# Where the moving operand of the 272-token matmuls begins within a 256-byte line

## What is computed

```python
h = concat([meta, x])                                                  # 272 tokens
h = h + 0.5 * rmsnorm(swiglu(rmsnorm(h, gn[0]), w_in[0], w_out[0]), gn[1])
h = h + rmsnorm(mlstm_mixer(rmsnorm(h, gn[2]), ...), gn[3])
h = h + 0.5 * rmsnorm(swiglu(rmsnorm(h, gn[4]), w_in[1], w_out[1]), gn[5])
return h[:, 16:]                                                       # 256 tokens
```

## Time and profile before

| what | value |
|---|---|
| median of three runs | 775.6 us (775.16 to 777.53) |
| the profiled execution's own time | 775.25 us |
| its span, first to last instruction | 773.4 us |
| TensorE busy | 765.1 us, 99% of the span |
| VectorE, ScalarE, GpSimd busy | 75%, 54%, 16% |
| mean granted TensorE clock | 0.998 of full speed |
| share of 16 DMA engines, weights' queue | 61.6% |

### The profile page before, as it was taken

One profiled execution on the slowest core, in us unless ns is written; L12 is line 12 of the kernel. 1 busy time (PEld: TensorE's weight loads), 2 busy tenths in 40 slices (PEclk: granted clock), 3 DMA queues, 4 the chain that ended last, 5 costly groups with the idle time before them and its releaser, 6 DMA issues.

```text
span 773.4 us, 14578 instructions
## 1 busy us (share of the span) xinstructions
PE 765.1 (99%) x5754; PEld 722.8 (93%) x5754; DVE 579.8 (75%) x926; ACT 417.2 (54%) x735; POOL 123.1 (16%) x140
## 2 busy tenths in 40 slices
PE   9999999999999999999999999999999999999997
PEld 9999999999999999889999998889999988999985
DVE  6877776699697887588888888677676768567663
ACT  7544444444357576495445443556655457455541
POOL 3800000032230002000000000010054411035510
PEclk9999999999999999999999999999999999999999
DMA  9867666696617564468888786735574571754541
GB/s 349 307 246 248 240 218 232 216 334 208 189 57 259 182 197 145 138 220 309 318 279 310 275 299 214 229 135 190 145 239 137 163 271 44 242 181 135 151 124 54
DMA packets 46402, 162.98 MB, mean 211 GB/s; under 512 B 5200, under 2 KB 6768, under 8 KB 46336
## 3 DMA queue, kind: packets, MB, share of 16 engines
q1 hardware_dynamic: 46336, 162.06, 61.6%
HBM read 160.96 MB, written 1.08 MB: 210 GB/s over the span
## 4 chain that ended last, share of the span: by engine, by line
PE 89%; DVE 5%; ACT 2%; issue 2%; DMA 1%; SPq 0%; POOL 0%; DVEq 0%; POOLq 0%; ACTq 0%
PE ps L374 21%; PE ps L375 20%; PE ps L376 20%; PE ps L824 5%; PE ps L826 5%; PE ps L825 5%; PE ps L766 3%; DVE w L1248 2%; PE ps L681 1%; DVE cv L1553 1%; PE ps L625 1%; PE ps L756 1%; ACT w L875 1%; PE ps L737 1%; PE ps L746 1%
## 5 line engine op out<-in xcount | busy, mean ns | idle before, releaser
L1248 DVE TENSOR_TENSOR w<-raw,w 128x1024 fp32r<-128x1024 f32 x237 | 287.9, 1222 | 124.5 <-ACT w L875 123.9
L374 PE MATMUL ps<-u,w 128*128 128x256 f32 (+1 forms) x1275 | 362.9, 285 | 0.3 <-DVE w L1248 0.3
L376 PE MATMUL ps<-u,w 128*128 128x256 f32 (+1 forms) x1275 | 358.4, 281 | 0.0
L375 PE MATMUL ps<-u,w 128*128 128x256 f32 (+1 forms) x1275 | 358.3, 281 | 0.0
L875 ACT CAST w<-raw 128x1024 fp32r<-128x1024 f32 x237 | 246.1, 1050 | 109.4 <-PE ps L376 77.7
L374 PEld LDWEIGHTS ps<-u,w 128*128 128x128 f32 x1275 | 239.9, 188 | 5.3 <-issue 3.1
L375 PEld LDWEIGHTS ps<-u,w 128*128 128x128 f32 x1275 | 239.9, 188 | 0.1
L376 PEld LDWEIGHTS ps<-u,w 128*128 128x128 f32 x1275 | 239.6, 188 | 0.0
L1948 POOL TENSOR_SCALAR Sb<-Sb,st 128x256 f32<-128x256 f32 x32 | 44.9, 1418 | 94.2 <-DVE st L1717 94.2
L1266 DVE SCALAR_TENSOR_TENSOR acc<-adr,cact,acc 128x1024 f32<-128x1024 f32 x42 | 55.7, 1339 | 0.0
L919 ACT ACTIVATE si<-tmp 128x272 f32<-128x272 f32 (+1 forms) x40 | 17.0, 426 | 65.9 <-DVE tmp L1361 65.9
(11 more groups left out here) (271 smaller groups left out, 982.5 us busy)
## 6 DMA issues: line engine op xcount, KB each, us to landing
raw<-wst SPq DMA_DIRECT2D x245, 512.0 KB, 4.5
adr<-wada SPq DMA_DIRECT2D x48, 512.0 KB, 3.7
Bt<-bias_rows SPq DMA_DIRECT2D x8, 192.0 KB, 3.7
hT<-xT SPq DMA_DIRECT2D x4, 272.0 KB, 4.5
hT<-xtok SPq DMA_DIRECT2D x2, 512.0 KB, 5.8
sq<-nrow SPq DMA_DIRECT2D x2, 512.0 KB, 4.9
g2row<-weight_rows SPq DMA_DIRECT2D x2, 512.0 KB, 6.3
sq<-weight_rows SPq DMA_DIRECT2D x2, 512.0 KB, 5.4
```

The lines of the kernel that those rows point to most:

```text
L374: e.matmul(out, a, x1, start=first, stop=False)
L375: e.matmul(out, a, x2, start=False, stop=False)
L376: return e.matmul(out, b, x1, start=False, stop=last)
L1248: e.tensor_tensor(b, r, a.bitcast(F32), ALU.subtract).then_inc(*tick(s_split, k))
```

## The change

In stages of 272 tokens the columns used are moved from 0..271 to 32..303 of each row, in `u1` and `u2` and in the first feed-forward's `h1` and `h2`. The moving operands of these matmuls then begin 128 bytes behind a multiple of 256, and the output-gate blocks, which leave out 16 columns, at 192 bytes. Stages of 256 tokens keep columns 48..303 (`LEAD` is still 48). No instruction is added, removed or reordered, and no tile changes its size or place.

```diff
-LEAD = 48
+LEAD_T = 32
+LEAD = LEAD_T + NMETA
...
-        for n, row in ((T, TP), (S, S)):
+        for n, row, lead in ((T, TP, LEAD_T), (S, S, 0)):
...
-            h1.append(sb(f"h1_{n}", [P, NF, row], F32R, fx)[:, :, 0:n])
+            h1.append(sb(f"h1_{n}", [P, NF, row], F32R, fx)[:, :, lead:lead + n])
...
-            h2.append(sb(f"h2_{n}", [P, NF, row], F32R, fx)[:, :, 0:n])
+            h2.append(sb(f"h2_{n}", [P, NF, row], F32R, fx)[:, :, lead:lead + n])
...
-                x1, x2 = u1[:, :, 0:T], u2[:, :, 0:T]
+                x1, x2 = u1[:, :, LEAD_T:LEAD_T + T], u2[:, :, LEAD_T:LEAD_T + T]
```

More of the change, by code:

```diff
@@ L888, in first_input @@
                     e.wait_ge(s_x[k // 2].handle, 16)
-                    e.mul(u1[:, k, 0:T], hT[:, k, :], norm_gain(0, k)).then_inc(*tick(s_u1, ("f0", k)))
+                    e.mul(u1[:, k, LEAD_T:LEAD_T + T], hT[:, k, :], norm_gain(0, k)).then_inc(*tick(s_u1, ("f0", k)))
                 split_to(1)
@@ L970, in normalised @@
                     e.wait_ge(*(read(("r2", s)) if k == KT - 1 else (s_tmp.handle, at(s_tmp, (s, k)))))
-                    e.copy(u1[:, k, 0:n], tmp[:, k % 4, 0:n]).then_inc(*tick(s_u1, ("a", k)))
+                    e.copy(u1[:, k, LEAD_T:LEAD_T + n], tmp[:, k % 4, 0:n]).then_inc(*tick(s_u1, ("a", k)))
                     if k == 1:
@@ L1313, in first_input @@
                     e.wait_ge(s_u1.handle, at(s_u1, ("f0", k)))
-                    e.scalar_tensor_tensor(u2[:, k, 0:T], hT[:, k, :], norm_gain(0, k), u1[:, k, 0:T].bitcast(F32), ALU.mult,
+                    e.scalar_tensor_tensor(u2[:, k, LEAD_T:LEAD_T + T], hT[:, k, :], norm_gain(0, k), u1[:, k, LEAD_T:LEAD_T + T].bitcast(F32), ALU.mult,
                                            ALU.subtract).then_inc(*tick(s_u2, ("f0", k)))
@@ L1458, in lower @@
                     e.wait_ge(s_u1.handle, at(s_u1, (nxt, k)))
-                    e.tensor_tensor(u2[:, k, 0:n], tmp[:, k % 4, 0:n], u1[:, k, 0:n].bitcast(F32), ALU.subtract).then_inc(
+                    e.tensor_tensor(u2[:, k, LEAD_T:LEAD_T + n], tmp[:, k % 4, 0:n], u1[:, k, LEAD_T:LEAD_T + n].bitcast(F32), ALU.subtract).then_inc(
                         *tick(s_u2, (nxt, k)))
```

## The result

| | before | after |
|---|---|---|
| median | 775.32 us (775.08 to 777.53) | 778.22 us (777.89 to 780.54), 13 runs |
| ratio | | 1.0035, 95% interval 1.0028 to 1.0042 |
| span of the execution read here | 773.4 us | 776.1 us |

The kernel became slower by 2.9 us (0.35%). That is 0.2 us above the range of the prediction, on the side of rival B.

What follows compares the result with a forecast made beforehand. TensorE's own rate was taken as the bound. The three terms summed to 0 against 775.6 us on the median; 775.4 us was put, a small step toward the output-gate blocks' possible gain, with range 764.8 to 778.0 us.

Steps and rivals of the forecast that it cites:

- the range of the prediction: Whole kernel: 764.8 to 778.0 us, said to hold 0.8 of the chance.
- rival B: First feed-forward and mLSTM projections: reads meet more often at 128 bytes, up to 6.0 us slower; chance 0.20 with rival C.
- the step that took zero for the 272-column matmuls: 1984 matmuls of 272 columns: rate unchanged, bounded by 9.7 us less and 6.0 us more.
- the upper level: 256-column stretches: 117.9 ns from start to start, against 113.4 at the lower; 272-column matmuls taken as at the upper per column.
- The last sentence of the prediction: 272-column matmuls: the prediction is wrong if they change their rate at all.
- The output gates: 192 matmuls going from 64 to 192 bytes: taken as zero, bounded by 0.7 us gained and 0.1 us lost.
- new wait for weights: If TensorE became faster, weights would be the next thing late; no gain given back at the 360 us stretch.
- the six shifted writers: Six instructions writing or reading the shifted columns: a few ns each under slack; estimate 1.4 us with the cover gone.
- rival C: Later 256-column stretches enter another level: 4.0 us lost or 0.8 gained; large flip shares 0.20 with rival B.
- Rival A: 272-column stretches fall to the lower level through a changed weight-operand relation: 765.2 to 765.9 us; chance 0.36, including 0.11 between.
- the upper bound of 3 ns: 272-column matmuls: if each took the longest single duration, 3 ns more each, 6.0 us in all.
- the third part: Cost of the six instructions on shifted columns, covered by ACT and DVE slack, about 0.47 and 0.73 of the time busy.

Runs made afterwards that it cites:

- the run again: The kernel after the change, profiled once more with no edit; 777.96 us.
- u160_h224: Against the kernel after: 272-token operands moved to 160 bytes for u and 224 for h, output-gate blocks at 224; 773.22 us.
- t192: Against the kernel after: 272-token operands u and h all moved to 192 bytes, output-gate blocks at 0; 772.56 us, ratio 0.996 to the kernel before.

## Why the prediction was wrong

**What failed** is the step that took zero for the 272-column matmuls: "A shift of 128 bytes thus leaves both levels where they were", and that their rate "points to their width rather than to their place". It set stretches at 64 bytes beside stretches at 192 and counted levels. The two counts were of blocks 24 matmuls long, right after an interruption, where seven of eight were at the upper level at either place. The long stretch at 192 bytes stood in the same table, at 113.4 ns, and no stretch of that length at 64 existed to set beside it. The weights' shift made one: 117.9 ns. So 64 and 192 do not look alike in a long stretch, and the comparison could not carry the conclusion. Even had it held for 256 columns, it said nothing of 272: there the rates by distance, from first to last start in a stretch, are

| distance in bytes | 0 | 64 | 128 | 160 | 192 | 224 |
|---|---|---|---|---|---|---|
| 272 columns, ns from start to start | 125.3 | 126.7 | 126.7 | 123.3 | 123.3 | 125.3 |

Six distances give three rates; 160 was seen on u and 224 on h only.

**The size.** The step bounded the price at -4.9 to +3 ns. What came, 126.66 against 125.33 ns over 1,420 steps on end, is +1.33 ns, inside the bounds and just past the 1.2 ns from which rival B was said to decide. 1984 x 1.33 = 2.6 us; 2.3 were seen from 16 to 266 us. Rival B, with its place (first feed-forward and mLSTM) and its test (under 793 matmuls in 25 to 125 us; 792 came), is what happened, at the low end of its price. Its reason, that two reads meet more often at 128 bytes, no run looked at. The last sentence of the prediction names this result as the one that would prove it wrong.

**The output gates** were taken at zero, with a bound of 0.7 us gained. They gained 0.5: their share at the upper level fell from seven of eight to two. The zero rested on the same counting, and was wrong for the same reason. That this gain would be given back by a VectorE instruction running beside GpSimd was in no part of the prediction; it cost 1.1 us at TensorE's new wait. The terms add up, 2.3 - 0.5 + 1.1 = 2.9 us. Without the wait the time would be some 777.1 us, inside the range, though the step on the 272 columns had failed just the same.

**What held.** TensorE's rate is the bound, the clock was not involved (1.00 in every stretch after as before), no new wait for weights came, the six shifted writers cost nothing that shows, and rival C's flip of the long 256-column run did not come (708 and 708). Rival A's premise, that the relation between weight tile and moving operand sets the level, was the right one with the wrong sign for 128 bytes. At 192 it is a gain: 813 instead of 800.

**A reading that misled.** The prediction wanted L375 on h to keep 284/288/291 if nothing changed. In the run again the answering row on tile h is

```profile
L376 PE MATMUL ps<-h,w x176: 287/288/292, 143.9 to 211.4; 128*128 128x272 f32 x176
```

The median did not move although the steps between starts grew by 1.33 ns; the shortest went from 284 to 287 and the longest from 291 to 292. Counts in a stretch show the rate; the single duration does not, so the upper bound of 3 ns, which was read from single durations, had no ground either. (A slip in the third part, on which nothing rests: 22 of 50 us is 0.44; the 0.47 is that of 25 to 125 us.)

By the page "TensorE: Matmul & The Clock Gate" of the Trainium skill (section "Step-by-step: what each phase is for") the weights' read port is independent of the moving operand's, so that loading weights takes nothing from a running matmul. The runs do not bear out that this makes the place indifferent: with instructions and clock unchanged, moving only the weights by 128 bytes took the u stretch from 800 matmuls to 792. By the page "SBUF — State Buffer" (section "🔬 SBUF: two separate sides") VectorE operations with two SBUF inputs and GpSimd operations that read SBUF lock each other out of a shared port pair; the subtraction's 0.41 us alone and 1.17 to 1.29 us beside GpSimd agree with that, and so does that each long one ends just behind an addition's end.

## What to carry to other kernels

Where TensorE's rate is the bound and one weight load goes with each matmul, treat the byte distance between weight tile and moving operand, within 256 bytes, as a tuning parameter, and measure it for each width by counting starts in a long stretch: here it was worth 113.4 against 117.9 ns in the long stretch of 256 columns and 123.3 against 126.7 at 272. A comparison of two places in the profile is only evidence if the stretches are alike in length, entry and width. A gain of half a microsecond on one engine can move two others into each other's way, so look at what the freed time now starts beside.

## What was not expected of the hardware

- At 272 columns the rate of a matmul stream depends on the distance between the places of its two operands (the table above), not on either place alone. At 256 columns the distance counts too (113.4 ns at 192 and 117.9 at 64 in the long stretch), but does not settle it: at 192 bytes 360 to 440 us has 113.4 ns and 655 to 677 us 117.9 in the same kernel.
- When the matmuls of a stream alternate between two places, three different pairs gave the same 124.4 ns, for 0 and 128 below the rates of both places.
- At 256 columns the output-gate blocks showed 117.9 to 118.7 ns at a distance of 224 (u160_h224) and 119.1 to 120.0 at 0 (t192), beside the two levels known from before.
- Each of the 17 long VectorE subtractions of 128x256 (1.16 to 1.29 us instead of 0.41) ended 0.28 to 0.29 us behind the end of a GpSimd addition; a weight split of 128x1024 took 1.91 us beside the additions and 1.23 without.
